# C's attention weights turned on VectorE and by DMA, and C's steps packed anew, in a hybrid attention layer on one Trainium2 core

## What is computed

```python
h = rms_norm(x, norm_pre)
qa, ka, va, ga, qb, kb, vb, gb, qc, kc, vc, gc = split(h @ w_in)
# A: 12 heads, stick-breaking attention over the whole past
# B: 12 query heads on 4 key heads, window of 128 keys, ALiBi, sinks
# C: 8 heads, own 64-token chunk and the 8 before it, relative bias, softmax
s = q @ k.T * 64 ** -0.5 + bias        # band of C: up to 5 blocks of 128 keys
p = softmax(where(visible, s, -1e30))
o = p @ v
mixed = concat(oa * silu(ga), ob * silu(gb), oc * silu(gc))
y = x + rms_norm(mixed @ w_out, norm_post)
```

## Time and profile before

| | us |
|---|---|
| median of 3 runs | 2088.51 |
| lowest and highest | 2088.03 and 2090.72 |
| the profiled execution, its own time | 2091.37 |
| its span, first to last instruction | 2089.7 |
| mean granted TensorE clock in it | 0.994 |
| unit c1's attention, 48 slots | 954 to 1071 of the span |

### The profile page before, as it was taken

How to read it: one execution, slowest core, us unless ns; L and a number is a source line. 1 busy time by engine, 2 the same in 40 slices (tenths; PEclk the granted TensorE clock), 3 DMA queues, 4 the chain that set the end, 5 groups by cost and what they waited for, 6 DMA issues and landing times.

```text
span 2089.7 us, 31323 instructions
## 1 busy us (share of the span) xinstructions
PE 2028.3 (97%) x13216; PEld 1838.8 (88%) x13216; DVE 1079.7 (52%) x2003; ACT 686.6 (33%) x1232; POOL 9.3 (0%) x28
## 2 busy tenths in 40 slices
PE   5999999999999999999999999999999999999997
PEld 4998988989898888999999999999999978887885
DVE  6457676776867677433334333444244563335234
ACT  5323333333333333323223232333223452232231
POOL 1000000000000000000000000000000000000000
PEclk9999999999999999999999999999999999999999
DMA  6256676576767676222131312222222353326523
GB/s 245 69 117 130 140 162 148 123 152 137 140 128 164 141 149 149 63 52 78 42 91 42 83 41 61 63 51 53 58 66 52 124 170 101 101 96 241 181 92 121
DMA packets 603012, 230.75 MB, mean 110 GB/s; under 512 B 395944, under 2 KB 577976, under 8 KB 601112
## 3 DMA queue, kind: packets, MB, share of 16 engines
q1 hardware_dynamic: 601704, 220.76, 42.3%
q0 software_dynamic: 1168, 7.99, 1.0%
HBM read 167.52 MB, written 64.37 MB: 111 GB/s over the span
## 4 chain that ended last, share of the span: by engine, by line
PE 80%; DVE 9%; DMA 3%; ACT 3%; SPq 2%; issue 2%; DVEq 0%; POOL 0%; ACTq 0%; POOLq 0%
PE ps L873 17%; PE ps L875 17%; PE ps L874 17%; PE ps L1080 5%; PE ps L1082 5%; PE ps L1081 5%; PE ps L964 3%; PE ps L1050 3%; DVE arena L1490 3%; PE ps L983 3%; PE ps L1021 2%; PE ps L931 2%; DVE arena L1484 1%; SPq L653 1%; DMA arena<-in_x_prompt_dram 1%
## 5 line engine op out<-in xcount | busy, mean ns | idle before, releaser
L873 PE MATMUL ps<-act_hi,w_hi 128*128 128x352 f32 x2688 | 883.4, 329 | 12.9 <-DVE arena L1425 7.2
L875 PE MATMUL ps<-act_hi,w_lo 128*128 128x352 f32 x2688 | 864.3, 322 | 0.0
L874 PE MATMUL ps<-act_lo,w_hi 128*128 128x352 f32 x2688 | 863.8, 321 | 0.0
L873 PEld LDWEIGHTS ps<-act_hi,w_hi 128*128 128x128 f32 x2688 | 505.5, 188 | 44.3 <-issue 29.2
L874 PEld LDWEIGHTS ps<-act_lo,w_hi 128*128 128x128 f32 x2688 | 506.5, 188 | 0.0
L875 PEld LDWEIGHTS ps<-act_hi,w_lo 128*128 128x128 f32 x2688 | 505.6, 188 | 0.0
L1401 DVE TENSOR_TENSOR w_lo<-w_raw,w_hi 128x512 fp32r<-128x512 f32 x348 | 237.2, 683 | 314.6 <-ACT w_hi L1241 216.1
L1169 ACT ACTIVATE w_hi<-w_raw 128x512 fp32r<-128x512 f32 x224 | 139.3, 624 | 222.2 <-DMA w_raw<-in_w_in_dram 222.0
L1080 PE MATMUL ps<-w_hi,act_hi 128*128 128x512 f32 x496 | 197.1, 397 | 4.2 <-DVE act_lo L1556 2.1
L1082 PE MATMUL ps<-w_hi,act_lo 128*128 128x512 f32 x496 | 195.8, 395 | 0.0
L1081 PE MATMUL ps<-w_lo,act_hi 128*128 128x512 f32 x496 | 195.8, 395 | 0.0
(11 more groups left out here) (141 smaller groups left out, 1734.8 us busy)
## 6 DMA issues: line engine op xcount, KB each, us to landing
w_raw<-in_w_in_dram SPq DMA_DIRECT2D x176, 256.0 KB, 3.1
w_raw<-in_w_out_dram SPq DMA_DIRECT2D x124, 256.0 KB, 2.8
weight_scratch<-arena SPq DMA_DIRECT2D x216, 128.0 KB, 3.8
arena<-weight_scratch SPq DMA_DIRECT2D x54, 512.0 KB, 4.4
w_raw<-in_w_in_dram SPq DMA_DIRECT2D x96, 128.0 KB, 2.5
arena<-in_x_prompt_dram SPq DMA_DIRECT2D x8, 1024.0 KB, 5.9
out_dram<-arena SPq DMA_DIRECT2D x14, 512.0 KB, 2.9
value_scratch<-arena SPq DMA_DIRECT2D x48, 132.0 KB, 3.4
```

Of the source, the lines that this page charges most:

```text
L873: mm(bank(g, GN), wh, ah, start=(k == 0), stop=False)
L874: mm(bank(g, GN), wh, al, start=False, stop=False)
L875: last = mm(bank(g, GN), wl, ah, start=False, stop=(k == KT - 1))
```

## The change

1. `by_blocks` holds for every step of C but the sample's: the weights are turned on VectorE (now L1594), sent out by four DMAs (now L674) and read back by one (now L680), with the same two scratches, made longer. PE's transposes and ScalarE's copies for these steps are gone. The values of a step are multiplied two steps later (`C_FLIGHT`), so that the last two steps of a unit end in the next unit.
2. C's tiles are packed as (4, 1), (5,), (3, 2), (6,), (7, 0), (TT,): 7, 5, 7, 5 and 6 blocks per head. The buffers `c_s` are now one per step in flight (1792 and 1280 columns, both heads in one), and the bias of C has a place of its own.
3. `tile_table` puts the key tile ahead of the gate tile for C's units too. The gate of a C unit is so computed 12 slots later.
4. The steps of units c1 to c3 begin at their slots' start; those of the last unit end 4 slots earlier.

```diff
             tiles.append(("q", u + 1))
-        if 0 < u < NA:
+        if 0 < u < NA + NC:
...
-BAND_STEPS = {"c": ((4, 1, 0), (3,), (5, 2), (6,), (7,), (TT,)), "b": ((0, 1), (2, 3), (4, 5), (6, 7), (TT,))}
-GROUP_END = {"a": (4, 8, 9), "c": (1, 4, 5), "b": (1, 3, 4)}
+BAND_STEPS = {"c": ((4, 1), (5,), (3, 2), (6,), (7, 0), (TT,)), "b": ((0, 1), (2, 3), (4, 5), (6, 7), (TT,))}
+GROUP_END = {"a": (4, 8, 9), "c": (1, 3, 5), "b": (1, 3, 4)}
 STEPS = {"a": len(A_STEPS), "c": len(BAND_STEPS["c"]), "b": len(BAND_STEPS["b"])}
...
         if runs and runs[-1][2] == P * m:
-            runs[-1][2] = P * m + P
+            runs[-1][2] = P * m + (P if m < TT else DEC)
         else:
...
     n = STEPS[kind]
-    begin, end = {"a": (0, 48), "c": (5 if i == 0 else 2, 48)}.get(kind, (0, SLOT_LEN[u]))
+    begin, end = {"a": (0, 48), "c": (5 if i == 0 else 0, 44 if i == NC - 1 else 48)}.get(kind, (0, SLOT_LEN[u]))
     if (kind, i, r) == ("b", 0, 0):
...
 FLIGHT = 3
-LAST_A = NA - 1
+C_FLIGHT = 2
+LAST_A, LAST_C = NA - 1, NA + NC - 1
...
-    return UNITS[u][0] == "a" and A_STEPS[i][0][0] < TT
+    kind = UNITS[u][0]
+    return kind != "b" and i + 1 < STEPS[kind]
...
     if kind == "c":
-        return START[u][n + 1] - 0.02 if n + 1 < STEPS[kind] else START[u][n] + 6
+        if n + C_FLIGHT < STEPS["c"]:
+            return START[u][n + C_FLIGHT] - 0.02
+        if u < LAST_C:
+            return START[u + 1][n + C_FLIGHT - STEPS["c"]] - 0.02
+        return START[u][n] + 12.2 if by_blocks(u, n) else max(values_at(u, n - 1) + 0.01, START[u][n] + 6)
     return next_start(u, n + 2) - 0.02
...
                 plan += [(s + 0.35 * pace(u, i), "biased", u, i), (s + pace(u, i), "normed", u, i)]
+                if by_blocks(u, i):
+                    plan.append((s + pace(u, i) + 0.9, "turn_weights", u, i))
         if kind != "a":
...
         if kind != "b":
-            plan += [(group_end_at(u, k) + 0.6, "mix", u, k) for k in range(3)]
+            plan += [(max(group_end_at(u, k) + 0.6, gate_at(u) + 2.5 + 0.1 * k), "mix", u, k) for k in range(3)]
         else:
...
-        else:
-            for i in range(STEPS["a"]):
-                if by_blocks(u, i):
-                    plan += [(START[u][i] + 5.6, "part_weights", u, i), (START[u][i] + 9.6, "load_weights", u, i)]
+        for i in range(STEPS[UNITS[u][0]]):
+            if by_blocks(u, i):
+                at = START[u][i] + {"a": 5.6, "c": 4.6}[UNITS[u][0]]
+                plan += [(at, "part_weights", u, i), (at + 4.0, "load_weights", u, i)]
...
-        ORIGIN, FLOATS = 16512, 53060
+        ORIGIN, FLOATS = 16512, 53208
...
         small = place("small", [P, 160], F32, 160)
-        arena = place("arena", [P, 13892], F32, 13892)
+        arena = place("arena", [P, 14232], F32, 14232)
...
         vc = arena[:, 9152:9664].rearrange("p (b c) -> p b c", b=4)
-        work = arena[:, 9664:13892]
+        work = arena[:, 9664:14232]
         stick = [work[:, 1024 * i:1024 * i + 1024] for i in range(FLIGHT)]
-        c_s = stick
-        c_bias = work[:, 2948:4228].rearrange("p (h c) -> p h c", h=2)
+        c_s = [work[:, 0:1792], work[:, 1792:3072]]
+        c_bias = work[:, 3072:4352].rearrange("p (h c) -> p h c", h=2)
...
         def part_no(u, i):
-            return (STEPS["a"] - 1) * u + i + 1
+            return STEP0[u] - u + i + 1
...
-            return u + 1 if u < NA else NA + STEP0[u] - STEP0[NA] + i + 1
+            return u + 1 if u < B0 else B0 + STEP0[u] - STEP0[B0] + i + 1
+        def weights_of(u, i):
+            if UNITS[u][0] == "a":
+                return stick[(STEP0[u] + i) % FLIGHT]
+            return c_s[i % 2][:, 0:2 * step_keys(u, i)]
...
-        wt_d = [nc.dram_tensor(f"weight_scratch{i}", (1024, P), F32, kind="Internal").ap() for i in (0, 1)]
+        wt_d = [nc.dram_tensor(f"weight_scratch{i}", (1792, P), F32, kind="Internal").ap() for i in (0, 1)]
         v_d = nc.dram_tensor("value_scratch", (TOK, P), F32, kind="Internal").ap()
...
+        def step_keys(u, i):
+            return sum(keys_of(u, m) for m in BAND_STEPS["c"][i])
         def score_place(u, m):
...
                 return b_s[(STEP0[u] + i) % 2][0:rows_of(m), h, c:c + n]
-            return c_s[h][0:rows_of(m), score_place(u, m):score_place(u, m) + n]
+            c = h * step_keys(u, i) + score_place(u, m)
+            return c_s[i % 2][0:rows_of(m), c:c + n]
...
-            return b_s[(STEP0[u] + i) % 2][:, h, 0:512] if UNITS[u][0] == "b" else c_s[h]
+            if UNITS[u][0] == "b":
+                return b_s[(STEP0[u] + i) % 2][:, h, 0:512]
+            return c_s[i % 2][:, h * step_keys(u, i):(h + 1) * step_keys(u, i)]
...
                 n = part_no(u, i)
-                s = stick[(STEP0[u] + i) % FLIGHT]
+                s = weights_of(u, i)
                 sp.wait_ge(wt_blocks, n)
...
                 for q in range(4):
-                    sp.dma_start(block_rows(wt_d[n % 2])[:, :, 32 * q:32 * q + 32], blocks(s[32 * q:32 * q + 32, :])).then_inc(wt_parted, 16)
+                    sp.dma_start(block_rows(wt_d[n % 2][0:s.shape[1]])[:, :, 32 * q:32 * q + 32], blocks(s[32 * q:32 * q + 32, :])).then_inc(wt_parted, 16)
...
                 sp.wait_ge(wt_parted, 64 * n)
-                sp.dma_start(stick[(STEP0[u] + i) % FLIGHT].rearrange("p (b c) -> p b c", c=P),
-                             wt_d[n % 2].rearrange("(b p) c -> p b c", p=P)).then_inc(wt_in, 16)
+                s = weights_of(u, i)
+                sp.dma_start(s.rearrange("p (b c) -> p b c", c=P),
+                             wt_d[n % 2][0:s.shape[1]].rearrange("(b p) c -> p b c", p=P)).then_inc(wt_in, 16)
...
                     if i == 0:
-                        assert (STEP0[u] - 1) % FLIGHT == 2
-                        sp.wait_ge(pv_done, STEP0[u] - FLIGHT)
+                        sp.wait_ge(toep_out, 16)
                     else:
...
                         continue
-                    if by_blocks(*last):
+                    if by_blocks(*last) and UNITS[last[0]][0] == "a":
                         pe.wait_ge(t_ready, step_no(*last))
+                    elif by_blocks(*last):
+                        pe.wait_ge(s_biased, head_no(last[0], BAND_STEPS["c"][last[1]][-1], side))
                     else:
...
                         zh = head_bank(u, i, h)
-                        if i + 1 < STEPS["c"]:
-                            nk = sum(keys_of(u, m) for m in BAND_STEPS["c"][i])
-                            last = fn(c_s[h][:, 0:nk], bank(zh, nk), ACT.Copy)
-                        else:
-                            fn(c_s[h][:, 0:4 * DEC], bank(zh, 4 * DEC), ACT.Copy)
-                            last = fn(c_s[h][0:DEC, 4 * DEC:5 * DEC], bank(zh, DEC, DEC, 4 * DEC), ACT.Copy)
+                        wt = turned_of(u, i, h)
+                        fn(wt[:, 0:4 * DEC], bank(zh, 4 * DEC), ACT.Copy)
+                        last = fn(wt[0:DEC, 4 * DEC:5 * DEC], bank(zh, DEC, DEC, 4 * DEC), ACT.Copy)
                         if h == 0:
...
-                dve.wait_ge(pv_done, max(STEP0[u], STEP0[u] + i - 1) if u == B0 else STEP0[u] + i - (kind == "b"))
+                dve.wait_ge(pv_done, max(STEP0[u], STEP0[u] + i - 1) if u in (NA, B0) else STEP0[u] + i - 1)
                 for m in BAND_STEPS[kind][i]:
...
                 elif what == "turn_weights":
-                    dve.wait_ge(w_ready, step_no(u, n))
-                    s = stick[(STEP0[u] + n) % FLIGHT]
+                    if UNITS[u][0] == "a":
+                        dve.wait_ge(w_ready, step_no(u, n))
+                    else:
+                        dve.wait_ge(p_normed, head_no(u, BAND_STEPS["c"][n][-1], 1))
+                    s = weights_of(u, n)
                     v.transpose(s, s).then_inc(wt_blocks, 1)
```

## The result

| | us |
|---|---|
| changed kernel, median of 4 runs | 2062.09 (2061.65 to 2064.22) |
| kernel before, 4 runs | 2088.72 (2088.03 to 2090.72) |
| ratio | 0.9875, 95% interval 0.9863 to 0.9887 |
| profiled execution, its own time and its span | 2062.3 and 2060.3 |
| mean granted clock in it | 0.993 |

The kernel became 26.6 us faster; the forecast was 2063.0, 25.4 us less. The page of the changed kernel shows where to look. Its PE row answers to the earlier trace rows, its groups of PE to the earlier trace rows.

The account below looks back on a forecast made before the run. PE, busy 97% of the span, was taken as the bound: 26.4 us from transposes, less 0.5 for product waits and 0.5 for the gate, gives 25.4 us, so 2088.51 becomes 2063 us, range 2060.5 to 2070.

Parts of the forecast that it names:

- Transposes: On PE in C's four units: 240 transposes removed at 0.11 us each, 26.4 us gained, 6.6 per unit.
- the rival of the recorded length: On PE in C: each removed transpose frees its recorded 0.276 us, 66 us in all, giving 2022; chance 0.02.
- The Trainium skill's price: On PE: the skill's page gives about 275 ns for one 128x128 transpose; the forecast used 0.11 us from starts.
- VectorE's turns: On VectorE in C: turning the weights adds 35.5 us, 8.9 per unit, making it busy 51.7 of 110.6 us.
- Waits for product results: In C, PE waits for VectorE to copy products out of PSUM: 0.5 us taken, bounds 0 to 8.8.
- two slots to spare: In C: the room in which product results can leave PSUM before PE waits; a slot is 2.30 us.
- The detour: In C, scores' start to returned turned weights: 27.0 to 31.8 us, inside 32.3; PE waits taken as 0.
- the worst sum for c3's first step: In unit c3: with the bias made ahead, the detour takes up to 33.4 us, 1.1 over the time available.
- SP's queue: In SP's queue: four issues out and one back added per step, with pieces of w_in behind; cost taken as 0.
- DMA share: In a C unit: the DMA engines' busy share rises from 0.24 to at most 0.60, under a4's 0.67.
- The gate: In C: gates made 12 slots later leave 1.5 us of margin in c3; cost 0.5 us, bounds 0 and 2.
- The rule against block turning: The skill names TensorE for a 128x128 transpose where PSUM will do; counted against the change, for late returning weights.

Follow-up runs that it names:

- run 2: The changed kernel with 12 dummy transposes put on PE ahead of the scores of each of C's 20 block-turned steps: 2090.84 us.
- run 5: The changed kernel with each of C's 20 turns on VectorE made three times, the turned weights released only after them: 2083.0 us.
- run 7: The changed kernel with 10 to 14 small VectorE copies behind each of C's turns, after the turned weights are released: 2074.84 us.
- run 3: The changed kernel without the move of the key tile in C, so gates come first as before: 2075.16 us.
- run 4: The changed kernel with C's gates first again and the store of mixed outputs 1.1 slots earlier in SP's list for c0, c1, c2: 2062.42 us.
- Run 8: The changed kernel with C's values one step after the scores instead of two, gates first, return asked for 1.9 slots after sending: 2230.23 us.

## Why the prediction was right

- **Transposes, 26.4 us.** Right, and run 2 excludes the rival of the recorded length (2022). The two stretches of C differ by 27.3 us, and from c1's first scores to c2's it is 6.88 us less where 6.6 was forecast: nearer to 0.115 us per transpose than to 0.11. The medians' gain, 26.6, agrees with both within its scatter.
- **The Trainium skill's price.** Its TensorE page (TensorE: Matmul & The Clock Gate, Part 4) gives about 275 ns for a transpose. The trace has 280 ns as recorded length and 0.12 us as cost; by an estimate from the page's figure run 2 would have taken 2062 + 66 = 2128 us, and it took 2090.84.
- **VectorE's turns.** The 20 of them were to take 35.5 us, and VectorE's time in c1 was to be 51.7; it was 51.20 of 110.60.
- **Waits for product results, 0.5 us (0 to 8.8).** The size was right, 0 measured in C, but the reason was not good. I read it from a busy share of 47%. Run 5 has 59% and waits of up to 3.5 us where a4 has 73% and 2.2 us in all. What decides is how long the chain ahead of one copy out of PSUM is, and run 7 gives the room that was left over the turn's own time: 1.6 us at the tightest step. The forecast had "two slots to spare", 4.6 us; with the turn's 2.04 the place at c0's third step had some 3.6. That a turn fitted at every place I had not worked out, so here the 0 was in part luck.
- **The detour, 27.0 to 31.8 us.** Those sums were for a step of 7 blocks; the longest detour measured was 27.8, and all 20 took 19.7 to 27.8. I scaled the way out by 1792 / 1024, to 9.4 to 14.2; it took 8.4 to 11.8 for the steps of 7 blocks. One 224 KB part lands in 4.8 us by the page where 128 KB take 3.8, so time grew by 1.26 where size grew by 1.75. The way back was 7.7 by scaling and 5.1 to 7.9 measured, and the worst sum for c3's first step, 33.4, also had 7.9 us up to the last scaling where 6.5 were needed. The two places named as the tightest, c3's first and fifth step, are the two tightest; the 1.1 us that might have been missing there were 3.1 to spare.
- **SP's queue, 0.** Right for the time, though the margin is not the 21 us by which pieces are asked for ahead: in run 5 3 to 4 us of later sending were enough for ScalarE to want a piece, and runs 3 and 4 differ by the order of this queue alone, and by 13 us.
- **DMA share, at most 0.60.** It was 0.63. I added shares of units of different lengths; the same rows as time give (0.24 x 117.2 + 0.43 x 118.1 x 60 / 72) / 110.6 = 0.64.
- **The gate, 0.5 us (0 to 2).** 0. But this is the step where the argument was thin: I costed the move of the gates as a risk only, and run 3 shows that without it 13 us of the gain are lost. With the unit's last values now ending in the next unit, the mixed outputs are stored later, and a gate tile in first place has to wait for that store; run 4 adds that it is the store's place behind a piece and the return of 896 KB that makes this wait long. The profile of before could not show it, since there the last values end in their own unit; the wait on `mix_stored` in the code of the gate's first copy could have been read.
- **The rule against block turning.** The Trainium skill (VectorE: DVE Perf Modes, Rules for kernel authors) names TensorE for a 128x128 transpose where PSUM will do as destination. Here TensorE is the bound and 26.6 us were gained by leaving it. Run 8 shows the condition: 20 detours of 19.7 to 27.8 us have to be behind other work.

## What to carry to other kernels

When one engine is busy 97% of the span without waits, an instruction's price is the distance of starts around it, and moving it to an engine with room gives that back, as it did here to within about 1 us in C, if the longer way has steps of flight enough. Ask for the length of the chain ahead of each copy that the bound engine needs, over the other queues too, and not for a busy share. And where a change lets work end later, look for everyone who reuses that work's buffer and for what stands ahead of its store: a wait that has never lasted is in no profile, but it is in the code.

## What the runs showed of the hardware

- A wait of PE can cost more than its length: behind 3.3 us idle the granted clock was at 0.50 and 19 steps of product matmuls took 5.7 us instead of 3.0, some 2.7 us lost; behind 3.8 us idle some 1.6 us were lost; after 1.5 us idle in the same kernel it stayed at 1.00.
- The same store landed 7.9 to 8.7 us after its issue (four of them) with a 256 KB piece of `w_in` and an 896 KB read of the DRAM scratch issued just ahead of it, 5.0 and 6.2 us with only the piece ahead, and 3.7 to 4.0 us (three of them) with both behind.
- A transfer of 224 KB in packets of 32 floats landed in 4.8 us where one of 128 KB takes 3.8.
